# Two more raw weight tiles, in the place of the normed tokens

## The reference

```python
def _moe(h, router, w_gate_up, w_down):
    logits = (h @ router).astype(jnp.float32)
    top_v, top_i = lax.top_k(logits, TOP_K)            # TOP_K = 2
    gates = jax.nn.softmax(top_v, axis=-1)
    gate_full = jnp.sum(jax.nn.one_hot(top_i, N_EXPERTS, dtype=jnp.float32) * gates[..., None], axis=-2)
    y = jnp.zeros_like(h)
    for e in range(N_EXPERTS):                         # 8 experts
        y = y + gate_full[..., e:e + 1] * _swiglu(h, w_gate_up[e], w_down[e])
    return y

def _swiglu(h, w_gate_up, w_down):                     # D_FF = 3584
    gu = h @ w_gate_up
    g, u = gu[..., :D_FF], gu[..., D_FF:]
    return (jax.nn.silu(g) * u) @ w_down
```

## Time and profile before

| | |
|---|---|
| median of three runs | 1550.06 us |
| the profiled execution, its own time | 1546.84 us |
| its span, first to last instruction | 1545.0 us |
| PE busy | 1489.3 us (96%) |
| DVE busy | 1169.0 us (76%) |
| ACT busy | 1001.6 us (65%) |
| loads on SP's queue (q1) | 453.93 MB |
| one load of an expert's tile, issue to landing, median | 13.3 us (gate and up), 12.7 us (down) |
| TensorE's granted clock, mean | 0.995 |

### The profile page before, as it was taken

How to read it: one execution, slowest core, us unless ns; L and a number is a source line. 1 busy time by engine, 2 the same in 40 slices (tenths; PEclk the granted TensorE clock), 3 DMA queues, 4 the chain that set the end, 5 groups by cost and what they waited for, 6 DMA issues and landing times.

```text
span 1545.0 us, 19275 instructions
## 1 busy us (share of the span) xinstructions
PE 1489.3 (96%) x7570; PEld 1213.7 (79%) x7570; DVE 1169.0 (76%) x1009; ACT 1001.6 (65%) x861; POOL 124.2 (8%) x130
## 2 busy tenths in 40 slices
PE   8999999999989999999999999998999999999995
PEld 6888888899979987788776888776887786887773
DVE  5555445464565466999899898999898998998996
ACT  5453444343463346777888876888776988777884
POOL 0000000013125031400000000000000000000000
PEclk9999999999999999999999999999999999999998
DMA  9655555566517642799999999999999999999994
GB/s 342 198 191 174 180 190 169 188 213 207 178 54 220 218 137 83 301 397 357 368 406 418 398 407 394 379 407 416 399 401 392 386 409 408 405 401 385 394 389 165
DMA packets 151119, 468.31 MB, mean 303 GB/s; under 512 B 9792, under 2 KB 15936, under 8 KB 138480
## 3 DMA queue, kind: packets, MB, share of 16 engines
q1 hardware_dynamic: 144720, 453.93, 78.8%
q0 software_dynamic: 2816, 9.96, 2.3%
q10 hardware_dynamic: 3488, 3.13, 0.6%
HBM read 459.62 MB, written 7.37 MB: 302 GB/s over the span
## 4 chain that ended last, share of the span: by engine, by line
PE 73%; DVE 10%; DMA 9%; ACT 3%; SPq 3%; issue 2%; DVEq 0%; ACTq 0%
DVE wlo L367 8%; DMA raw<-in_m_w_gate_up_dram 6%; PE bY L383 6%; PE bY L385 6%; PE bY L384 6%; PE bS L385 6%; PE bS L384 6%; PE bS L383 6%; PE bG L383 4%; PE bU L383 4%; PE bU L385 4%; PE bU L384 4%; PE bG L384 4%; PE bG L385 4%; SPq L435 3%; DMA raw<-in_m_w_down_dram 2%
## 5 line engine op out<-in xcount | busy, mean ns | idle before, releaser
L367 DVE TENSOR_TENSOR wlo<-raw,whi 128x2048 fp32r<-128x2048 f32 x426 | 967.9, 2291 | 214.5 <-ACT whi L361 212.7
L361 ACT ACTIVATE whi<-raw 128x2048 fp32r<-128x2048 f32 x426 | 812.1, 1915 | 314.7 <-PE bS L385 114.4
L966 PE MATMUL bY<-whi,hTh 128*128 128x512 f32 x224 | 92.1, 411 | 13.6 <-DVE wlo L367 12.9
L383 PE MATMUL bY<-whi,hTh 128*128 128x512 f32 x224 | 89.9, 401 | 0.0
L384 PE MATMUL bY<-whi,hTl 128*128 128x512 f32 x224 | 89.2, 398 | 0.0
L385 PE MATMUL bY<-wlo,hTh 128*128 128x512 f32 x224 | 89.2, 398 | 0.0
L967 PE MATMUL bY<-wlo,hTh 128*128 128x512 f32 x224 | 88.9, 397 | 0.0
L966 PE MATMUL bS<-whi,eTh 128*128 128x512 f32 x192 | 76.3, 397 | 0.0
L967 PE MATMUL bS<-wlo,eTh 128*128 128x512 f32 x192 | 76.2, 397 | 0.0
L383 PE MATMUL bS<-whi,eTh 128*128 128x512 f32 x192 | 76.1, 396 | 0.0
L384 PE MATMUL bS<-whi,eTl 128*128 128x512 f32 x192 | 76.1, 396 | 0.0
(11 more groups left out here) (458 smaller groups left out, 3139.3 us busy)
## 6 DMA issues: line engine op xcount, KB each, us to landing
raw<-in_m_w_gate_up_dram SPq DMA_DIRECT2D x224, 1024.0 KB, 13.3
raw<-in_m_w_down_dram SPq DMA_DIRECT2D x112, 1024.0 KB, 12.7
raw<-in_b_w_in_dram SPq DMA_DIRECT2D x36, 1024.0 KB, 5.1
raw<-in_f_w_gate_up_dram SPq DMA_DIRECT2D x28, 1024.0 KB, 5.2
raw<-in_f_w_down_dram SPq DMA_DIRECT2D x14, 1024.0 KB, 5.0
raw<-in_a_w_out_dram SPq DMA_DIRECT2D x4, 1024.0 KB, 14.9
biasrev<-toeplitz SPq DMA_DIRECT2D x32, 128.0 KB, 5.1
raw<-in_b_w_out_dram SPq DMA_DIRECT2D x4, 1024.0 KB, 5.1
```

The source lines that it names most:

```text
L361: nc.scalar.activation(whi[:, h], raw[:, r], ACT.Copy).then_inc(hi_done, 1)
L367: nc.vector.tensor_tensor(wlo[:, r], raw[:, r], whi[:, h].bitcast(F32), ALU.subtract).then_inc(lo_done, 1)
L383: pe.matmul(dst, a[0], b[0], start=start, stop=False)
L966: pe.matmul(backward(banks[s], 0, 512), xs[:, kb], w[0], start=kb == 0, stop=False)
```

## The change

`RAW` stays 9, and `MORE` = 2 slots are added, `raw_more` and `wlo_more`, in the memory of `hnh` and `hnl`. Until tile 98 the slots go round as before; from tile `T_MORE` = 99 they go round 11. The first load to each of the two new slots waits for the first expert tile to have been used (`T_MOE + 1`), after which nothing in the unrolled program reads `hnh` or `hnl`; every other load waits for the tile that last had its slot. The overflow loop takes the tokens back from `hn_dram` to slot 7 of `raw`, ScalarE and VectorE split them to slots 8 and 7 of `wlo`, and its `gather` reads these.

```diff
+MORE = 2
...
         top[0] = phase
+        at_hnh = top[0]
         hnh = place("hnh", [NT, D], F32R)
         hnl = place("hnl", [NT, D], F32R)
+        end_hnl, top[0] = top[0], at_hnh
+        raw_more = place("raw_more", [MORE, 2048], F32)
+        assert top[0] == end_hnl
+        top[0] = at_hnh
+        wlo_more = place("wlo_more", [MORE, 2048], F32R)
...
+        def in_order(t, item):
+
+            return t + item * FFN_TILES
+
+        T_MORE = -(-T_MOE // RAW) * RAW
+
+        def ring(t):
+
+            return t % RAW if t < T_MORE else (t - T_MORE) % (RAW + MORE)
+
+        fills = [0] * (RAW + MORE)
+        filled, before_it = [], []
+        owner = [None] * (RAW + MORE)
+        for t in range(T_MOE + E * FFN_TILES):
+            fills[ring(t)] += t > 0
+            filled.append(fills[ring(t)])
+            before_it.append(owner[ring(t)])
+            owner[ring(t)] = t
...
+        def free_count(t, item):
+
+            if isinstance(item, int):
+                last = before_it[in_order(t, item)]
+                return T_MOE + 1 if last is None else last + 1
+            return used_count(t, item, OVER_RAW)
+
+        raw_of = lambda r: raw[:, r] if r < RAW else raw_more[:, r - RAW]
+        wlo_of = lambda r: wlo[:, r] if r < RAW else wlo_more[:, r - RAW]
...
-            nc.scalar.activation(whi[:, h], raw[:, r], ACT.Copy).then_inc(hi_done, 1)
+            nc.scalar.activation(whi[:, h], raw_of(r), ACT.Copy).then_inc(hi_done, 1)
...
-            nc.vector.tensor_tensor(wlo[:, r], raw[:, r], whi[:, h].bitcast(F32), ALU.subtract).then_inc(lo_done, 1)
+            nc.vector.tensor_tensor(wlo_of(r), raw_of(r), whi[:, h].bitcast(F32), ALU.subtract).then_inc(lo_done, 1)
...
-                sp.wait_ge(tile_used, used_count(t_all, n, RAW if isinstance(n, int) else OVER_RAW))
+                sp.wait_ge(tile_used, free_count(t_all, n))
...
                 with sp.If(m < m_last):
+                    sp.wait_ge(hn_out, 32)
+                    sp.wait_ge(tile_used, count((m, 1, E), FFN_TILES, T_MOE))
+                    sp.dma_start(raw[:, OVER_RAW].rearrange("p (t d) -> p t d", t=NT),
+                                 hn_dram.rearrange("(t p) d -> p t d", p=P)).then_inc(back_full, 16)
...
                 with act.If(m < m_last):
+                    act.wait_ge(back_full, count((m, 1, 0), 16, 16))
+                    copy(wlo[:, OVER_RAW + 1], raw[:, OVER_RAW], back_hi)
```

More of the change, by code:

```diff
@@ L234, in encoder @@
         c_in = [sem(f"const{i}") for i in range(15)]
-        raw_full = [sem(f"raw_full{i}") for i in range(RAW)]
+        raw_full = [sem(f"raw_full{i}") for i in range(RAW + MORE)]
+        back_full, back_hi, back_lo = sem("back_full"), sem("back_hi"), sem("back_lo")
         over_full = [sem(f"over_full{i}") for i in range(OVER_RAW)]
@@ L332, in load_x @@
                              x_in[0].rearrange("(m a) d -> a m d", a=4)[a][:, sl]).then_inc(x_in_done[kh], 16)
+        def in_order(t, item):
[11 more added lines that the diff above has]
+            owner[ring(t)] = t
         def slots(t, item=0):
             if isinstance(item, int):
-                t += item * FFN_TILES
-                return t % RAW, t % HI
+                t = in_order(t, item)
+                return ring(t), t % HI
             return (t - T_MOE) % OVER_RAW, (t - T_MOE) % HI
@@ L343, in full_count @@
             if isinstance(item, int):
-                t += item * FFN_TILES
-                return raw_full[t % RAW], 16 * ((t - 1) // RAW + 1)
+                t = in_order(t, item)
+                return raw_full[ring(t)], 16 * filled[t]
             t -= T_MOE
             register, step, _ = item
-            return over_full[t % OVER_RAW], count((register, step, 0), 16 * (FFN_TILES // OVER_RAW), 16 * (t // OVER_RAW + 1))
+            loads = len(range(t % OVER_RAW, FFN_TILES, OVER_RAW))
+            return over_full[t % OVER_RAW], count((register, step, 0), 16 * loads, 16 * (t // OVER_RAW + 1))
         def used_count(t, item, depth):
             if isinstance(item, int):
-                return max(t + item * FFN_TILES - depth + 1, 0)
+                return max(in_order(t, item) - depth + 1, 0)
             return count(item, FFN_TILES, max(t - depth + 1, T_MOE))
+        def free_count(t, item):
[5 more added lines that the diff above has]
+        wlo_of = lambda r: wlo[:, r] if r < RAW else wlo_more[:, r - RAW]
         def make_hi(act, t, item=0):
@@ L366, in make_lo @@
             dve.wait_ge(hi_done, count(item, FFN_TILES, t + 1))
-            nc.vector.tensor_tensor(wlo[:, r], raw[:, r], whi[:, h].bitcast(F32), ALU.subtract).then_inc(lo_done, 1)
+            nc.vector.tensor_tensor(wlo_of(r), raw_of(r), whi[:, h].bitcast(F32), ALU.subtract).then_inc(lo_done, 1)
         def wblk(t, b):
             r, h = slots(t)
-            return whi[:, h, b * 512:b * 512 + 512], wlo[:, r, b * 512:b * 512 + 512]
+            return whi[:, h, b * 512:b * 512 + 512], wlo_of(r)[:, b * 512:b * 512 + 512]
         def backward(t, first, width):
@@ L378, in wblk_backward @@
             r, h = slots(t, item)
-            return backward(whi, h * 2048 + b * 512, HI * 2048), backward(wlo, r * 2048 + b * 512, RAW * 2048)
+            low = backward(wlo, r * 2048 + b * 512, RAW * 2048) if r < RAW else backward(
+                wlo_more, (r - RAW) * 2048 + b * 512, MORE * 2048)
+            return backward(whi, h * 2048 + b * 512, HI * 2048), low
         def mm3(pe, dst, a, b, start, stop):
@@ L426, in load_expert @@
                     t -= FFN_TILES
-                sp.wait_ge(tile_used, used_count(t_all, n, RAW if isinstance(n, int) else OVER_RAW))
+                sp.wait_ge(tile_used, free_count(t_all, n))
                 gu, dn = m_w_gate_up[0, one(e)], m_w_down[0, one(e)]
                 src = expert_tile(gu.rearrange("o k n -> (o k) n"), dn.rearrange("o k n -> (o k) n"), t, by_half)
-                dst = raw[:, slots(t_all, n)[0]]
+                dst = raw_of(slots(t_all, n)[0])
                 if t < SINGLE:
@@ L835, in _, with gather @@
             pe.matmul(Y1[:, 2 * E:4 * E], tri[:, 1], chosen, start=True, stop=True).then_inc(rank_psum, 1)
-            def gather(n, rounds):
+            def gather(n, rounds, high=hnh, low=hnl):
                 for r in rounds:
-                    bank, src = (G, U, T, X)[r], (hnh, hnl)[r // 2]
+                    bank, src = (G, U, T, X)[r], (high, low)[r // 2]
                     for kk in range(4):
@@ L1053, in _ @@
                     pe.wait_ge(pick_ready, count((m, 1, 0), 1, E + 1))
-                    gather(0, range(4))
+                    pe.wait_ge(back_hi, count((m, 1, 0), 1, 1))
+                    pe.wait_ge(back_lo, count((m, 1, 0), 1, 1))
+                    gather(0, range(4), *(wlo[:, r].rearrange("p (t d) -> p t d", t=NT) for r in (OVER_RAW + 1, OVER_RAW)))
                     pe.wait_ge(x_added, count((m, 1, 0), 2, 2))
@@ L1982, in _ @@
                     pick(of_item, (m, 1, E), full_slots)
+                    dve.wait_ge(back_hi, count(over, 1, 1))
+                    lo(wlo[:, OVER_RAW], raw[:, OVER_RAW], wlo[:, OVER_RAW + 1], back_lo)
                     for t in range(CUT):
```

## The result

The changed kernel takes 1532.66 us (median of four runs, 1531.02 to 1533.79), the kernel before on the same chip 1550.1 (four runs, 1550.02 to 1550.2): ratio 0.9887, 95% interval 0.987 to 0.9904. The profiled execution took 1533.53 us, its span 1531.6, which is 13.4 less than the span of before.

The account below looks back on a forecast made before the run. Half items were taken to wait for data that could come earlier only from low-rate ends of full items. Recoverable 6.0 + 2.3 + 1.9 + 1.9 = 12.1 us off the 1550.1 median gave 1538.0, range 1533.5 to 1547.

Parts of the forecast that it names:

- 940 to 978: (412 - 387) / 412 x 38 = 2.3 us: End of the full item 2: time lost by loads at 387 instead of 412 GB/s, recoverable with two more slots, 2.3 us.
- the two of 1.9: Full items' ends, 1165 to 1202 and 1390 to 1427: 391 instead of 412 GB/s, 1.9 us recoverable at each.
- q0's adding: Low-rate slices just behind the low stretches (290 GB/s, 750 to 758): adding to `acc_dram`, same cost wherever it lies, left out.
- my own account: Items 1 to 7: lead gained at full items' ends, capped at 6.0 us, spent on half items' waits; 12.1 us used.
- The first full item's 6.0: 694 to 750, at 359 GB/s: 7.2 us lost, of which 6.0 us taken as recoverable because issues move by 6.0.
- At most all waits, 16.1 us: Upper end of the gain: all data waits in the half items 1, 3, 5 and 7 vanish, 16.1 us.
- Landings of 9 to 11 us: Sign of being right: loads at the end of full items land after 9 to 11 us instead of 5.1.
- near 400: Sign of being right: the first full item's end, 694 to 750, moves near 400 GB/s, where it moved 359.
- the engines were not dry: Rival: DMA share, 0.98 to 1.01 in low stretches, is the measure, so only 3.3 us gained, 1546.8; chance 0.10.
- Only the first full item: Rival: later low stretches come from something other than a full ring, leaving 6.0 us gain, 1544.1; chance 0.13.
- No gain at all: Rival: another memory limit, as by the 358 GB/s rule, holds the low stretches; 1550.1 us, chance 0.05.
- The late gather (1563.2): Slower rival: GpSimd's token gather queues behind the deeper ring, 8.4 us late in items 1, 3, 5; 1563.2, chance 0.05.

Follow-up runs that it names:

- the extra loads: Four unused 1024 KB loads added to the kernel before: at full items' ends 1550.56 us, mid half items 1559.24; at full items' ends in the changed kernel 1537.28.
- the ring's sizes: Kernel before with eight slots instead of nine, 1557.06 us; changed kernel with ten instead of eleven, 1535.6; with twelve, 1.26% better than the kernel before.
- the unused slots: Changed kernel with its ring left at nine slots, so the two new slots are never used: 1547.02 us, ratio 0.9989 to the kernel before.
- the second execution: The changed kernel, unedited, timed and profiled once more: 1533.16 us (5 runs) against 1550.32 for the kernel before.

## Why the prediction was right and wrong

**The mechanism held.** Half items waited for data and the data could come earlier only from the ends of full items. Both sides were tried: the extra loads and the bytes show the gaps, the ring's sizes show what they are worth, the unused slots exclude the rest of the edit.

**The step that failed is the size of the later full items' terms**, "940 to 978: (412 - 387) / 412 x 38 = 2.3 us" and the two of 1.9. They were to measure all that a full item's end loses, and one such end is worth 3.7 to 4.0 us, measured. The stretches were cut too short: I left out the slices behind as q0's adding, but the low stretch of item 6's end goes on behind 1427, where 13 us lose 1.1 us beside the same adding. The full rate that I set against it was too low too: 415 GB/s were to be had for my 412, which makes the 1.9 into 2.1. Together with 0.2 us ahead of the stretch the bytes account for 3.4; the last half microsecond stays open. Put through my own account with 4.0 for each, the lead is 6.0 at item 1, back at its cap of 6.0 at the items 3, 5 and 7, and the use is 3.3 + 2.9 + 2.4 + 6.0 = 14.6. The experts' part in the traces is 14.8 us shorter, and 15.0 in the second execution.

**Term by term, saved in the half items:** item 1, 3.3 predicted and 3.0 measured; item 3, 2.9 and 3.0; item 5, 2.4 and 2.2; item 7, 3.5 and 6.2. So the waits of the earlier trace rows were a good price for the first three, and all the shortfall of the sum stands in item 7, where it was the stock that was counted too small. The first full item's 6.0 wasn't put to the test by the times: with ten slots, where it is 3.0 at most, item 1 saves the same 3.0. The landings say a little less than 6.0: the load of item 1's tile 12 lands 21.5 us behind the item's start, 5.0 earlier than before, and 5.2 in the second execution.

**The upper end wasn't one.** "At most all waits, 16.1 us" took 412 GB/s and VectorE's waits as limits. With eleven slots the rest of the half item moves 415 GB/s, and the kernel with twelve has its experts' part 17.7 us shorter than before, 8.6 of it in item 7 with its 7.5 us of wait. The full rate read from a kernel with a short ring is itself a little lower.

**The median.** 17.4 us by the medians stand against 13.4 by the spans and 14.8 in the experts' part. I took 12.1 from a median of three runs that lay within 0.2 us. In two other series 23 runs each of the same kernel spread over 8.2 and 6.0 us (medians 1548.94 and 1550.32), and both profiled executions of before (1546.84, 1547.38) lie below these. With 14.6 for 12.1 the forecast would have been 1535.5, inside the range, and still 2.8 above what was measured. The traces show two things that vary. The experts begin between 595.2 and 599.2 us in the twelve traces, at 595.9 in the one on which I worked and at 597.3 and 597.9 in the changed kernel's. And with nine slots the items 1, 3 and 5 take 106.1 to 107.4 us from one trace to the next, where with ten to twelve they take 103.9 to 104.0. So the 14.8 counts from an execution that is among the shortest in both. Which part of the 2.6 us between 14.8 and 17.4 that explains stays open, and so does whether the changed kernel varies less as a whole (1531.02 to 1535.21 in nine runs).

**The signs I named.** y_out of the items 2 and 4: 970.3 and 1192.7, 222.4 us apart, where about 222.5 was expected. VectorE's waits of 0.8 in the items 1, 3 and 5: right. Item 7's about 4: it is 2.1. Landings of 9 to 11 us: the load of the first tile of the items 3, 5 and 7 takes 10.8, 10.0 and 9.7, but that of item 1 takes 7.9, and the sign was set against the wrong base: these loads took 7.3, 7.6, 7.2 and 5.8 before, not 5.1. Twelve microseconds later all are shorter (8.3, 7.7, 7.3 and 6.3 for the items' tiles 4), and in the second execution loads issued just as item 1 begins land after 4.9 and 5.0 again. So this sign came in part. 390 GB/s for "near 400": the first full item begins with nearly no lead and doesn't fill both slots.

**The rivals.** That the engines were not dry (1546.8) falls by the extra loads, which cost at most a part of their transfers. Only the first full item (1544.1) falls by the eleven slots from item 6 on, which work without it. No gain at all fell with the time. The Trainium skill ("DMA: Bandwidth & Descriptors", Bandwidth, "Where 436 GB/s comes from") has about 358 GB/s for a core, worked out there as a half of a stack's 716. The trace of this core, which runs alone, disagrees: 414 over 68 us in the changed kernel. The late gather (1563.2) did not come: it lands 10.4 us after its issue for 10.5 before. The loads of `raw` issued from 1036 to 1058 take 15.2 us (median) for 16.4 before, so two more slots made no deeper backlog at that place, and the gather overtakes the one there is. The Trainium skill (same page, Queues, rings and completion order) has each engine take turns between its queues, and by that the gather doesn't wait for the ring; the trace agrees, with 10.4 us beside 15.2.

## What to carry to other kernels

When a kernel alternates between stretches that compute bounds and stretches that loads bound, count the ring's lead as a stock with a cap (slots times the pace), a refill and a use for each cycle, and find the refill from the whole cycle's bytes, not from the slices that look low. Stretches of two kernels have to be set by where the items begin, not by the time since the kernel's start: here a fixed stretch read 373 GB/s where the same part of the item had 398. An extra load of no use, put once where the ring is full and once where it isn't, shows in one pair of runs whether there are gaps that a slot could use. A slot is worth something in every cycle until the other engine bounds it, and from there only where the stock still runs out.

## What the runs showed of the hardware beside that

- The DMA busy share doesn't show gaps of this kind: 0.97 with 343 GB/s from 720 to 746 before, 1.00 with 377 after. The bytes do.
- GpSimd's issue of the indirect adds (`summed`) can be held for 10 us or more. Two views of 780 to 1000, before and in the changed kernel (ns min/median/max):

```profile
L546 POOL DMA_INDIRECT summed<-y_out,to_rows x3: 1527/1567/1765, 853.7 to 973.7; - x3
L590 POOL DMA_INDIRECT summed<-y_out,to_rows x3: 1567/1603/12448, 849.5 to 971.7; - x3
```

  In the changed kernel three of the ten issues take 10.2 to 12.5 us, one at the end of each of the items 1, 3 and 5, and the others 1.4 to 1.7 as before, so that the mean is 4.6 for 1.6. With twelve slots the mean is 4.7, but with ten it is 1.6, with eleven from item 6 on 1.6, and in the changed kernel with the extra loads 2.4. What holds them isn't shown. GpSimd has the time here (busy 151.5 of 1531.6 us); elsewhere this might be a price of more than ten slots.
- The rate of a stretch that loads bound rose a little with the ring: from 789 to 852 it is 412 GB/s with nine slots in two traces, 415 and 414 with eleven, 418 with twelve; with ten it is 415 as well.
